# First stack's two inner norms: column sums with ones as the stationary operand, and the power over 512 columns on GpSimd

## The reference, cut to what matters

```python
def rms_norm(x, g):
    xf = x.astype(jnp.float32)
    y = xf * lax.rsqrt(jnp.mean(xf * xf, axis=-1, keepdims=True) + EPS)
    return (y * g.astype(jnp.float32)).astype(x.dtype)

for l in range(DEPTH):                       # first stack, DEPTH = 2
    hn = rms_norm(h, g_mix[l])               # norm 0 of the layer
    ...                                      # attention and recurrent mixer, added to h
    hm = rms_norm(h, g_mlp[l])               # norm 1
    h = h + jnp.square(jax.nn.relu(hm @ w_mlp_in[l])) @ w_mlp_out[l]
    gate = jax.nn.sigmoid(rms_norm(h, g_ple[l]) @ w_ple_gate[l])   # norm 2
    h = h + gate * (p[l] @ w_ple_proj[l])
```

## Time and profile before

| | |
|---|---|
| runs, us | 2650.09, 2646.34, 2648.98 |
| median | 2648.98 |
| profiled execution | 2649.76 |
| span of its instructions | 2648.0 |
| PE busy | 2436.3 us, 92% |
| DVE busy | 1516.7 us, 57% |
| ACT busy | 835.7 us, 32% |
| POOL busy | 350.3 us, 13% |
| mean granted TensorE clock | 0.962 |

### The profile page before, as it was taken

One profiled execution on the slowest core, in us unless ns is written; L12 is line 12 of the kernel. 1 busy time (PEld: TensorE's weight loads), 2 busy tenths in 40 slices (PEclk: granted clock), 3 DMA queues, 4 the chain that ended last, 5 costly groups with the idle time before them and its releaser, 6 DMA issues. The chain is left out here.

```text
span 2648.0 us, 29239 instructions
## 1 busy us (share of the span) xinstructions
PE 2436.3 (92%) x11390; PEld 1955.5 (74%) x11398; DVE 1516.7 (57%) x2122; ACT 835.7 (32%) x1155; POOL 350.3 (13%) x219
## 2 busy tenths in 40 slices
PE   7988999998998899999888897999979889899996
PEld 5866888887786688888765676888856567688885
DVE  6774544455687445445478856444447984744544
ACT  4454222233435322223232343222223234322221
POOL 1011000000201100001024512000022541200002
PEclk9999999999999999999889998999989999899998
DMA  4211222221221132222121211222212111122222
GB/s 146 104 49 58 92 91 99 105 96 67 92 88 64 48 112 96 95 95 96 48 88 50 78 37 60 100 101 100 89 55 89 64 64 48 62 98 96 95 95 79
DMA packets 33301, 217.75 MB, mean 82 GB/s; under 512 B 4128, under 2 KB 4384, under 8 KB 7840
## 3 DMA queue, kind: packets, MB, share of 16 engines
q1 hardware_dynamic: 33184, 216.18, 23.1%
HBM read 214.07 MB, written 2.10 MB: 82 GB/s over the span
## 5 line engine op out<-in xcount | busy, mean ns | idle before, releaser
L323 PE MATMUL ps<-gh,wh 128*128 128x512 f32 (+1 forms) x1728 | 699.3, 405 | 109.3 <-DVE gl L464 65.4
L323 PE MATMUL ps<-gl,wh 128*128 128x512 f32 (+1 forms) x1728 | 681.9, 395 | 0.0
L323 PE MATMUL ps<-gh,wl 128*128 128x512 f32 (+1 forms) x1728 | 681.6, 394 | 0.0
L307 ACT ACTIVATE wh<-wr 128x2048 fp32r<-128x2048 f32 x196 | 374.0, 1908 | 560.2 <-PE ps L323 560.0
L313 DVE TENSOR_TENSOR wl<-wr,wh 128x2048 fp32r<-128x2048 f32 x172 | 394.8, 2295 | 248.9 <-ACT wh L307 248.9
L323 PE MATMUL ps<-hh,wh 128*128 128x512 f32 x1280 | 504.7, 394 | 7.4 <-DVE hl L944 3.1
L323 PE MATMUL ps<-hh,wl 128*128 128x512 f32 x1280 | 499.8, 390 | 0.0
L323 PE MATMUL ps<-hl,wh 128*128 128x512 f32 x1280 | 499.3, 390 | 0.0
L323 PEld LDWEIGHTS ps<-gh,wh 128*128 128x128 f32 (+1 forms) x1728 | 328.7, 190 | 211.0 <-DVE gl L464 72.7
L323 PEld LDWEIGHTS ps<-gl,wh 128*128 128x128 f32 (+1 forms) x1728 | 328.4, 190 | 72.8 <-issue 5.3
L323 PEld LDWEIGHTS ps<-gh,wl 128*128 128x128 f32 (+1 forms) x1728 | 328.0, 190 | 72.0
(11 more groups left out here) (204 smaller groups left out, 2414.4 us busy)
## 6 DMA issues: line engine op xcount, KB each, us to landing
wr<-in_weights SPq DMA_DIRECT2D x198, 1024.0 KB, 4.7
x<-in_xt SPq DMA_DIRECT2D x1, 2048.0 KB, 11.8
out_yt<-x SPq DMA_DIRECT2D x1, 2048.0 KB, 7.2
tmp<-in_positions SPq DMA_DIRECT2D x4, 256.0 KB, 3.3
arena<-in_gates SPq DMA_DIRECT2D x2, 512.0 KB, 4.8
arena<-in_embed SPq DMA_DIRECT2D x2, 512.0 KB, 5.6
par<-in_params_b SPq DMA_DIRECT2D x2, 274.0 KB, 3.1
par<-in_params_a SPq DMA_DIRECT2D x2, 157.5 KB, 2.7
```

Of the source, the lines that this page charges most:

```text
L307: act.activation(mem.wh[:, c % 2, :], mem.wr[:, c % 2, :], ACT.Copy).then_inc(sem["high"], 1)
L323: done = pe.matmul(out, stationary, moving, start=(first and n == 0), stop=(last and n == 2), skip_group_check=True)
```

## The change

For norms 1 and 2 of the two layers of the first stack, four functions are replaced:

- PE: sum_squares_wide makes two matmuls with a 128x128 block of ones as stationary operand and 512 columns of squares as moving operand (acc, then tile 7). The sums then stand on all partitions. It is issued at the same place, after the first product tile. The spread after the second product tile is gone.
- DVE: mean_square_wide works on 128x512 from PSUM and writes rb. The diagonals are gone.
- POOL: one_over_root_wide raises rb to -0.5 in place, in four instructions of 128x128, and raises "kept".
- ACT: the copy is gone.

```diff
+def sum_squares_wide(pe, mem, sem, n):
+
+    pe.wait_ge(sem["mean"], n)
+    pe.wait_ge(sem["gathered"], GATHERS * (n + 1))
+    pe.matmul(mem.ps[:, 4, :], mem.cst[:, C_ONES:C_ONES + P], mem.acc, start=True, stop=False, skip_group_check=True)
+    pe.wait_ge(sem["squared"], KT * (n + 1))
+    pe.matmul(mem.ps[:, 4, :], mem.cst[:, C_ONES:C_ONES + P], mem.sq[:, 1, :], start=False, stop=True,
+              skip_group_check=True).then_inc(sem["summed"], 1)
+
+
+def mean_square_wide(dve, mem, sem, n):
+
+    dve.wait_ge(sem["summed"], n + 1)
+    dve.tensor_scalar(mem.rb[:, :], mem.ps[:, 4, :], 1.0 / D, EPS, ALU.mult, ALU.add).then_inc(sem["mean"], 1)
+
+
+def one_over_root_wide(pool, mem, sem, n):
+    pool.wait_ge(sem["mean"], n + 1)
+    half = mem.cst[:, C_MHALF:C_MHALF + 1].broadcast_to([P, P])
+    for i in range(QT):
+        last = pool.tensor_tensor(mem.rb[:, P * i:P * (i + 1)], mem.rb[:, P * i:P * (i + 1)], half, ALU.pow)
+    last.then_inc(sem["kept"], 1)
...
                 for n in (1, 2):
                     gather_squares(pool, mem, sem, n)
-                    one_over_root(pool, mem, sem, n)
+                    one_over_root_wide(pool, mem, sem, n)
...
                 split_high(act, mem, sem, A_MLP + 1, a_used(A_MLP + 1))
-                keep_root(act, mem, sem, 1)
...
                 split_high(act, mem, sem, A_GATE + 1, a_used(A_GATE + 1))
-                keep_root(act, mem, sem, 2)
...
                 split_low(dve, mem, sem, A_MLP + 1)
-                mean_square(dve, mem, sem, 1)
-                root_diagonals(dve, mem, sem, 1)
+                mean_square_wide(dve, mem, sem, 1)
                 dve.wait_ge(sem["kept"], 2)
...
                 split_low(dve, mem, sem, A_GATE + 1)
-                mean_square(dve, mem, sem, 2)
-                root_diagonals(dve, mem, sem, 2)
+                mean_square_wide(dve, mem, sem, 2)
                 dve.wait_ge(sem["kept"], 3)
...
                 def after_first(tile):
                     if tile == A_TILE[A_MLP]:
-                        sum_squares(pe, mem, sem, 1)
-                    if tile == A_TILE[A_MLP] + 1:
-                        spread_root(pe, mem, sem, 1)
+                        sum_squares_wide(pe, mem, sem, 1)
...
                 def after_gate(tile):
                     if tile == A_TILE[A_GATE]:
-                        sum_squares(pe, mem, sem, 2)
-                    if tile == A_TILE[A_GATE] + 1:
-                        spread_root(pe, mem, sem, 2)
+                        sum_squares_wide(pe, mem, sem, 2)
```

## The result

The changed kernel takes 2952.93 us (median of four runs, 2951.3 to 2953.76) against 2648.82 before (four runs): the ratio is 1.1151, with a 95% interval of 1.1137 to 1.1166. That is 304 us more. The prediction said 3046 us, with a range of 2660 to 3085 and slower as the likely sign.

What follows compares the result with a forecast made beforehand. PE was taken to bound the kernel behind both norms; POOL's powers delay its low part: 2 x (96.3 + 2.6 + 97.2 + 2.6) = 397.4 us on 2649.76 gives 3047.2, median 0.8 lower, so 3046 us; range 2660 to 3085.

Steps and rivals of the forecast that it cites:

- PE's three spare tiles: Norms 1 and 2: PE has three more tiles to do, so it does not notice DVE idling for rb.
- the low part that meets PE: DVE's low part behind both drains gates PE's next chunk but one; slack 0.97 us at norm 1, 1.33 at norm 2.
- The cover: Time the four powers may take before PE waits: up to 8.2 us at norm 1, 7.2 at norm 2.
- The sum for the loss: Four norms: PE loses 96.3 us at norm 1, 97.2 at norm 2, 2.6 per restart; 397.4 us over two layers.
- The power on POOL: Four powers on 128 columns at norms 1 and 2: 0.205 us start, 0.204 us a column, 105.3 us a norm.
- The bounds: POOL's four powers at each norm: 5.1 us from below (ordinary two-input slope), 130.8 us from above (all by the column).
- the case of a partly fixed price: Rival on POOL's power: half of 817 ns is start, half by column; 54.7 us a norm, 2844 us; chance 0.33.
- the two signs: POOL's line of the 128x128 power: near 26 us each shows the linear price, 10 to 20 the partly fixed one.
- the linear price: POOL's power paid by the column: 3046 us, own range 2990 to 3085, wider 2950 to 3085; chance 0.47.
- PE's sums: Two wide matmuls: 1.72 us at full clock in place of 1.79, about 3.4 at half; they end when they did.
- The restart at the half clock: PE after each of the four waits: matmuls run at the lower clock, 2.6 us each, called likely.
- The first rival: POOL's power is a fixed price: four take 5.1 us, PE gains 3.6, 2645.4 us; chance 0.17.

Runs made afterwards that it cites:

- The power alone: Kernel before with only the change's four powers of 128x128 added on POOL, on the old contents of rb: 2971.25 us beside 2649.4 before.
- the powers on 16 columns: Changed kernel with its four powers on 16 columns each in place of 128, other columns left without root: 2669.03 us.
- filling the waits: Changed kernel with unread matmuls in PE's four waits, 336 at norm 1 and 331 at norm 2: 2946.8 us against 2953.6 not filled.
- without the price: Changed kernel with one power on 4 columns in place of the four on 128, other columns left without root: 2640.19 us, ratio 0.9969.

## Why the prediction was right, and by how much it was off

What bounds the kernel. Right: PE's three spare tiles and the low part that meets PE. With the measured 82.8 us in place of 105.3 the prediction's own steps give 96.3 - 22.5 = 73.8 us at norm 1 and 97.2 - 22.5 = 74.7 at norm 2. The traces have 354.17 - 280.14 = 74.0, and for norm 2 151.6 less the 76.9 with which it was entered (its sums start at 688.86 us and not at 611.99), 74.7. The power alone and the powers on 16 columns confirm the path. The cover, which is what the four powers may take before PE waits, was put at 8.2 us for norm 1 and 7.2 for norm 2. Measured, as the powers' time less the wait, it is 5.4 to 6.5 us and 7.3 to 7.4 us, in the changed kernel and with 16 columns alike: at norm 1 PE is through with its tiles earlier than the prediction had it, since the clock was low for a shorter time (6.4 and 6.5 us of cover) or not at all (5.4). The sum for the loss counts from where the tile stood before and does not use this number.

The power on POOL is the step that was mis-sized. Prediction: 0.205 us to start and 0.204 us a column, 105.3 us a norm. Measured: 0.386 us and 0.159 us a column, 82.8 us. The 0.8 us that 4 columns cost above a multiply were not all arithmetic by the column: 0.18 us are paid once. Four norms by 22.5 us are 90 us, and 3046 - 90 = 2956 against 2953 measured. The bounds held, and the case of a partly fixed price was the one that happened, with about a fifth of the 0.8 us fixed, so near the linear end of it. A row of 20.7 us stood between the two signs that the prediction had named (26 us for its own step, 10 to 20 for the partly fixed price), and 2953 us lies below the linear price's own range, 2990 to 3085, and just inside its wider one, from 2950: that the share paid once was only a fifth could not be read from any row of the kernel before, and is luck.

PE's sums. Right as a sum: they cost 690.80 - 688.86 - 0.23 = 1.71 us at norm 2, where 1.72 was forecast, and at norm 1 they ended when they did before (the mean starts at 261.40 against 261.33). Wrong in a point that the wait hid: I left the low stretch behind them as it was, and it was shorter or absent. In the changed kernel it is no gain, since PE only stops earlier.

The restart at the half clock. Expected 2.6 us for each wait, measured 1.7 as a mean of four by filling the waits (6.8 us in all). With this term as measured too the sum is 2956 - 4 x 0.9 = 2952 us.

The first rival's 2645.4 us, had the price been a fixed one, would have been some 4 us too high: without the price 7.7 us are gained, of which 3.6 us are the sum's, with the clock behind norm 1 as the likely but unproven place of the rest.

The Trainium skill (GPSIMD Engine Reference, section "Elementwise — side-by-side cycle accounting") measures its 2.6 cycles an element on an add and calls them the floor that reading two inputs sets. The prediction read them as going for any operation, and that does not hold for the power: 0.159 us a column are 191 cycles at the page's 1.2 GHz, an estimate by that page. The measurement decides.

The Trainium skill (GPSIMD Engine Reference, section "Architecture") gives each of eight cores 16 partitions and 16 lanes. That the cores work side by side agrees with the powers on 16 and on 128 partitions, 20.71 and 20.72 us. Whether a core takes its 16 partitions at once in a power these two runs cannot tell, since each fills all 16.

## What to carry to other kernels

A power on POOL is paid by the column and, from 16 to 128 partitions, not by the partition, so a factor for each token belongs on the partitions (4 columns) for the power, and may be spread afterwards; a layout that saves a spread of 0.86 us on PE can cost 82 us on another engine. Before an operation that a trace shows on 4 columns is widened to 512, time it by itself at two widths: one width can't tell a start from a slope. And ask where the late result meets the bounding engine: here it had 5.4 to 6.5 us of cover at norm 1 and 7.3 at norm 2, and each us beyond it cost its full length four times over.

## What the runs showed of the hardware that was not expected

The reciprocal on DVE takes 3.35 us for 128x512, nearly five times the 0.69 us of a multiply of that shape, and is still 24 times cheaper than the power on POOL.

After waits of PE of 3.0 to 6.2 us the granted clock fell to its lower level (eight waits in two kernels), and after those of 0.5 and 1.3 us, behind filled waits, it did not. A fall needs no long wait either: in the kernel before, the longest wait of PE in the 8 us ahead of norm 1 is 1.2 us, and the clock fell there. Ahead of norm 1 it fell in some executions and not in others, of the changed kernel too. When it fell, it stayed low for about 6.8 us behind the small sums and for about 3.4 us behind the wide ones; why the two differ no run here shows.
